# The last two output slabs by token halves, the norm by pairs of chunks, and the next stage's second slab split last

## What is computed

```python
x = x + gate_m * y
h = rmsnorm(x, norm_ffn_g[layer]) * (1.0 + scale_f) + shift_f
x = x + gate_f * swiglu(h, ffn_w_gate[layer], ffn_w_up[layer], ffn_w_down[layer])
```

## Time and profile before

| | us |
|---|---|
| median of three runs | 2349.04 (2347.94 to 2349.14) |
| the profiled execution's own time | 2349.4 |
| its span, first to last instruction | 2347.6 |

### The profile page before, as it was taken

The page is one execution under the profiler, slowest core; times in us unless marked ns, Lnnn a source line. Parts: engine busy times, 40 slices in busy tenths (PEclk is TensorE's granted clock), DMA queues, the critical chain, the costliest instruction groups (busy, mean ns, idle before and its releaser), DMA issues.

```text
span 2347.6 us, 34925 instructions
## 1 busy us (share of the span) xinstructions
PE 2266.1 (97%) x14369; PEld 1920.9 (82%) x14369; DVE 1401.0 (60%) x1800; ACT 1042.5 (44%) x1568; POOL 366.7 (16%) x164
## 2 busy tenths in 40 slices
PE   6999999999999999999999999999999999999998
PEld 4777888878889986668998998888777788898897
DVE  4856755543347765547883676645367345984484
ACT  4546553443215444435552455334255325553352
POOL 0346447347790000000000000000000000000000
PEclk9999999999999999999999999999999999999999
DMA  7433232334452324311333233212211222233232
GB/s 294 143 116 135 100 135 91 118 115 181 181 210 90 109 73 163 130 67 54 109 108 117 83 124 110 85 62 72 90 55 56 89 90 72 91 108 126 90 108 90
DMA packets 40762, 260.56 MB, mean 111 GB/s; under 512 B 4432, under 2 KB 6832, under 8 KB 10416
## 3 DMA queue, kind: packets, MB, share of 16 engines
q1 hardware_dynamic: 40624, 258.59, 30.3%
HBM read 256.42 MB, written 2.15 MB: 110 GB/s over the span
## 4 chain that ended last, share of the span: by engine, by line
PE 79%; DVE 8%; ACT 5%; issue 2%; POOL 2%; DMA 0%; DVEq 0%; ACTq 0%
PE D L301 10%; PE D L303 10%; PE D L302 10%; PE D L1638 7%; PE D L1640 7%; PE D L1639 7%; PE D L1403 2%; PE D L2866 2%; PE D L1405 2%; PE D L1404 2%; DVE lo L366 1%; PE D L2868 1%; PE D L2867 1%; PE D L1422 1%; ACT hi L362 1%
## 5 line engine op out<-in xcount | busy, mean ns | idle before, releaser
L366 DVE TENSOR_TENSOR lo<-raw,hi 128x2048 fp32r<-128x2048 f32 (+3 forms) x131 | 288.9, 2205 | 200.4 <-ACT hi L362 200.2
L362 ACT ACTIVATE hi<-raw 128x2048 fp32r<-128x2048 f32 (+3 forms) x131 | 230.1, 1756 | 328.6 <-PE D L303 240.0
L301 PE MATMUL D<-hH,lo 128*128 128x512 f32 x560 | 227.3, 406 | 5.6 <-DVE lo L366 5.6
L303 PE MATMUL D<-hH,hi 128*128 128x512 f32 x560 | 220.9, 394 | 0.0
L302 PE MATMUL D<-hL,hi 128*128 128x512 f32 x560 | 220.9, 394 | 0.0
L1638 PE MATMUL D<-tH,lo 128*128 128x256 f32 x768 | 216.3, 282 | 0.5 <-issue 0.5
L1640 PE MATMUL D<-tH,hi 128*128 128x256 f32 x768 | 216.3, 282 | 0.0
L1639 PE MATMUL D<-tL,hi 128*128 128x256 f32 x768 | 216.2, 282 | 0.0
L375 POOL TENSOR_TENSOR adar<-adar 128x1024 f32<-128x1024 f32 (+2 forms) x120 | 213.2, 1777 | 9.4
L373 POOL TENSOR_TENSOR adar<-adar,small 128x2048 f32<-128x2048 f32 x40 | 154.0, 3850 | 326.5 <-DVE zi L1289 189.0
L1638 PE MATMUL D<-hH,lo 128*128 128x256 f32 x576 | 162.6, 282 | 2.3 <-ACT D L1721 2.3
(11 more groups left out here) (537 smaller groups left out, 5481.7 us busy)
## 6 DMA issues: line engine op xcount, KB each, us to landing
raw<-in_slabs SPq DMA_DIRECT2D x185, 1024.0 KB, 4.8
adar<-in_ada SPq DMA_DIRECT2D x42, 1024.0 KB, 4.8
fw<-in_ada SPq DMA_DIRECT2D x6, 1024.0 KB, 24.0
x<-in_xin SPq DMA_DIRECT2D x2, 1024.0 KB, 8.9
dt<-bcast SPq DMA_DIRECT2D x8, 256.0 KB, 3.2
dtb<-bcast SPq DMA_DIRECT2D x8, 256.0 KB, 3.5
qd<-bcast SPq DMA_DIRECT2D x8, 256.0 KB, 3.7
out<-x SPq DMA_DIRECT2D x8, 256.0 KB, 2.2
```

The source lines that it names most:

```text
L301: T_.matmul(o, lo[s.slot][:, w], H[:, k, :], start=(k == 0), stop=False)
L303: last = T_.matmul(o, hi[s.slot][:, w], H[:, k, :], start=False, stop=(k == kc - 1))
L362: S_.activation(hi[s.slot][:, 0:n], raw[s.slot][:, 0:n], ACT.Copy).then_inc(hi_ready, 1)
L366: V_.tensor_tensor(lo[s.slot][:, 0:n], raw[s.slot][:, 0:n], hi[s.slot][:, 0:n], ALU.subtract).then_inc(lo_ready, 1)
```

## The change

The last two output slabs of each end (numbers 2 and 3) run by halves, in the order: slab 2 first half, slab 3 first half, slab 2 second half, slab 3 second half. Adds, squares and folds of these slabs go by halves. The sum of the first half stands in slab 2's second half, after 18 of its 48 matmuls, and takes four ones products instead of three. The norm goes by eight pairs of chunks: VectorE multiplies a pair by the root alone, ScalarE applies gain and shift as scale and bias, two activations to hH and two to tR, and tR is written wherever n is not 4; VectorE subtracts hH from tR. At n = 4 there is no tR, and VectorE makes hL chunk by chunk. The first next slab is split inside the norm (behind pair 0 on ScalarE, and behind the adds of slab 2's second half on VectorE). The second is split behind the last pair on both engines. A dummy slab that was loaded and split at the very end is gone. The cut diff (the counters of semaphores are left out):

```diff
-                    pe.wait_ge(h_ready, h_base(hb) + h * KC + k + 1)
+                    pe.wait_ge(h_ready, h_base(hb) + (h * KC + k) // 2 + 1)
...
-                T_.matmul(o, ones, a[:, 0, TH[h]], start=True, stop=False)
                 for m in range(2):
-                    pe.wait_ge(fsq_ready, 10 * f + 6 + 2 * h + m + 1)
+                    T_.matmul(o, ones, a[:, m, TH[h]], start=(m == 0), stop=False)
+                for m in range(2):
+                    pe.wait_ge(fsq_ready, 12 * f + 4 * h + m + 7)
                     last = T_.matmul(o, ones, b[:, m, TH[h]], start=False, stop=(m == 1))
...
             for h in range(2):
...
+                for j in range(N_OUT - 2, N_OUT):
+                    s = Slab(base + j)
+                    if h == 0:
+                        pe.wait_ge(lo_ready, s.plus(1))
+                        pe.wait_ge(bank_free[s.slot], s.prior())
+                    for m in range(2):
+                        o = D[s.slot][:, h, m * HT:(m + 1) * HT]
+                        for k in range(kc):
+                            if (h, j, m * kc + k) == (1, N_OUT - 2, 6):
+                                ones_half(pe, f, 0)
...
+        def half_fold_dve(dve, f, h):
+            dve.wait_ge(fsq_ready, 12 * f + 4 * h + 6)
+            dve.wait_ge(fold_ready, 3 * f + 1)
+            for a, b in sums_of(f):
+                last = V_.tensor_tensor(a[:, :, TH[h]], a[:, :, TH[h]], b[:, :, TH[h]], ALU.add)
+            last.then_inc(fold_ready, 1)
...
+        of_pair = lambda t_, p: t_[:, 2 * (p % 4):2 * (p % 4) + 2, TH[p // 4]]
+        norm_pair = lambda p: nq[:, 2 * (p % 2):2 * (p % 2) + 2, :]
+        whole_pair = lambda p: tR[:, (3, 1, 0, 2)[p // 2], 2 * (p % 2):2 * (p % 2) + 2, :]
+
+        def close_act(act, base, f, n, gain, shift):
+            def pair(p):
+                act.wait_ge(xg_ready, XG[n] + p + 1)
+                for to in (of_pair(hH, p), whole_pair(p)) if n != 4 else (of_pair(hH, p),):
+                    for m in range(2):
+                        c = 2 * (p % 4) + m
+                        last = S_.activation(to[:, m, :], norm_pair(p)[:, m, :], ACT.Identity, bias=shift(c), scale=gain(c))
+                last.then_inc(hh_ready, 1)
             S_.preload_act_table_set("natural_log_exp_and_others")
+            half_squares_act(act, base, f, 0, N_OUT - 1)
             half_rstd_act(act, f, n, 0)
+            pair(0)
+            split_hi(act, Slab(base + N_OUT))
+            half_squares_act(act, base, f, 1, N_OUT - 2)
+            pair(1)
+            pair(2)
+            half_squares_act(act, base, f, 1, N_OUT - 1)
+            pair(3)
+            half_rstd_act(act, f, n, 1)
+            for p in range(4, KC):
+                pair(p)
+            split_hi(act, Slab(base + N_OUT + 1))
...
+            def normed(p):
+                if p >= 2:
+                    dve.wait_ge(h_ready, hb0 + p - 1)
+                V_.tensor_tensor(norm_pair(p), of_pair(x, p), nrs[:, TH[p // 4]].unsqueeze(1).to_broadcast([P, 2, HT]),
+                                 ALU.mult).then_inc(xg_ready, 1)
+
+            def rest(p):
+                dve.wait_ge(hh_ready, hb0 + p + 1)
+                if n != 4:
+                    V_.tensor_tensor(of_pair(hL, p), whole_pair(p), of_pair(hH, p), ALU.subtract).then_inc(h_ready, 1)
...
             half_rstd_dve(dve, n, 0)
+            normed(0)
+            normed(1)
+            rest(0)
+            half_adds_dve(dve, base, gate, f, 1, N_OUT - 2)
+            split_lo(dve, Slab(base + N_OUT))
+            half_fold_dve(dve, f, 1)
+            normed(2)
+            rest(1)
+            normed(3)
+            rest(2)
+            half_adds_dve(dve, base, gate, f, 1, N_OUT - 1)
+            rest(3)
+            half_rstd_dve(dve, n, 1)
+            normed(4)
+            normed(5)
+            rest(4)
+            normed(6)
+            rest(5)
+            normed(7)
+            rest(6)
+            rest(7)
             split_lo(dve, Slab(base + N_OUT + 1))
...
         def last_dve(dve, base, gate, f, n, gain):
...
+            half_rstd_dve(dve, n, 0)
+            scaled(0, range(0, 4))
+            half_adds_dve(dve, base, gate, f, 1, N_OUT - 2)
+            half_fold_dve(dve, f, 1)
+            scaled(0, range(4, KC))
+            half_adds_dve(dve, base, gate, f, 1, N_OUT - 1)
+            half_rstd_dve(dve, n, 1)
+            scaled(1, range(KC))
...
-            alone(G_ROUT, N_SLABS + 1 - G_ROUT)
+            alone(G_ROUT, N_SLABS - G_ROUT)
```

More of the change, by code:

```diff
@@ L282, in build @@
         TH = (slice(0, HT), slice(HT, T))
-        BY_HALF = (2, 3, 5, 6, 8)
-        h_base = lambda hb: sum(2 * KC if b in BY_HALF else KC for b in range(hb)) + (4 if hb > 2 else 0) + (4 if hb > 5 else 0)
-        XG = {0: 0, 1: KC, 2: 3 * KC + 4, 3: 5 * KC + 4, 4: 7 * KC + 8, "x": 9 * KC + 8, 6: 10 * KC + 8, 7: 12 * KC + 12}
+        h_base = lambda hb: KC * hb + (4 if hb > 2 else 0) + (4 if hb > 5 else 0)
+        XG = {0: 0, 1: KC, 2: 2 * KC + 4, 3: 3 * KC + 4, 4: 4 * KC + 8, "x": 5 * KC + 8, 6: 6 * KC + 8, 7: 7 * KC + 12}
         RM = {0: 0, 1: 2, 2: 6, 3: 10, 6: 14, 7: 18}
@@ L594, in final_pe @@
         def final_pe(pe, base, kc, H, L, ready, f, begun=False):
-            for j in range(N_OUT - 1):
+            for j in range(N_OUT - 2):
                 s = Slab(base + j)
@@ L600, in final_pe @@
                     product(pe, s, kc, 2, H, L)
-            s = Slab(base + N_OUT - 1)
-            pe.wait_ge(lo_ready, s.plus(1))
-            pe.wait_ge(bank_free[s.slot], s.prior())
             for h in range(2):
[L605 to L614, removed]
+                for j in range(N_OUT - 2, N_OUT):
[8 more added lines that the diff above has]
+                                ones_half(pe, f, 0)
+                            w = slice((k * 2 + m) * P, (k * 2 + m + 1) * P)
+                            T_.matmul(o, lo[s.slot][:, w], H[:, k, TH[h]], start=(k == 0), stop=False)
+                            T_.matmul(o, hi[s.slot][:, w], L[:, k, TH[h]], start=False, stop=False)
+                            last = T_.matmul(o, hi[s.slot][:, w], H[:, k, TH[h]], start=False, stop=(k == kc - 1))
+                    last.then_inc(slab_done if h else out_half, 1)
         def square_sum(f, to, m, c, cols):
@@ L640, in final_dve @@
                 split_lo(dve, s.next(2))
[L641 to L662, removed]
+            dve.wait_ge(fsq_ready, 12 * f + 4)
+            for a, b in sums_of(f):
+                last = V_.tensor_tensor(a[:], a[:], b[:], ALU.add)
+            last.then_inc(fold_ready, 1)
+            half_adds_dve(dve, base, gate, f, 0, N_OUT - 2)
+            half_fold_dve(dve, f, 0)
+            half_adds_dve(dve, base, gate, f, 0, N_OUT - 1)
         def half_rstd_act(act, f, n, h):
@@ L691, in close_act @@
             S_.preload_act_table_set("natural_log_exp_and_others")
-            half_squares_act(act, base, f, 0)
+            half_squares_act(act, base, f, 0, N_OUT - 1)
             half_rstd_act(act, f, n, 0)
[L694 to L708, removed]
+            pair(0)
@@ L725, in close_dve @@
-        def close_dve(dve, base, gate, f, n, hb, gain, shift):
-            half_adds_dve(dve, base, gate, f, 0)
-            half_rstd_dve(dve, n, 0)
[L729 to L754, removed]
@@ new lines, in close_dve @@
+        def close_dve(dve, base, gate, f, n, hb, gain, shift):
+            hb0 = h_base(hb)
+            def normed(p):
[7 more added lines that the diff above has]
+                    V_.tensor_tensor(of_pair(hL, p), whole_pair(p), of_pair(hH, p), ALU.subtract).then_inc(h_ready, 1)
+                else:
+                    dve.wait_ge(xg_ready, XG[n] + p + 1)
+                    for m in range(2):
+                        c = 2 * (p % 4) + m
+                        last = V_.scalar_tensor_tensor(out=hL[:, c, TH[p // 4]], in0=norm_pair(p)[:, m, :], scalar=gain(c),
+                                                       in1=hH[:, c, TH[p // 4]], op0=ALU.mult, op1=ALU.subtract)
+                    last.then_inc(h_ready, 1)
+            half_rstd_dve(dve, n, 0)
+            normed(0)
[19 more added lines that the diff above has]
+            rest(7)
@@ L3279, in _ @@
             final_act(act, G_ROUT, 4)
-            close_act(act, G_ROUT, 4, 6, zero)
+            close_act(act, G_ROUT, 4, 6, col(vec, V["ln2"]), zero)
             quick_act(act, G_FFN2, 2, 5)
```

72 lines of the change are left out of this document (45 added, 27 removed).

## The result

The changed kernel takes 2359.23 us (median of six runs, 2356.55 to 2361.78) against 2349.09 us for the kernel before (six runs, 2347.53 to 2350.48): a ratio of 1.0045, 95% interval 1.0032 to 1.0058. It is slower by 10.1 us; 9.0 was forecast. Its profiled execution took 2361.1 us with a span of 2359.3.

What follows compares the result with a forecast made beforehand. ScalarE's queue was taken to bound the norm's second half at the ends feeding tR. 3 x 1.8 + 3.9 - 0.1 - 0.2 = +9.0 us gave 2358.0 against the median 2349.04; range 2349.5 to 2361.5.

Steps and rivals of the forecast that it cites:

- The operand: Norm activations on ScalarE get scale beside bias: second per-partition operand costs 0.08 us, step 0.48 instead of 0.40.
- f = 3: Fourth of five stage hand-overs: head wins 1 us, tail gives it back; 47.3 before, 47.2 after, -0.1.
- Rival (a): Second operand on ScalarE's activations is free: +0.9 in sum, 2349.9 us; chance 0.17, with half prices between.
- Rival (b): Back-to-back activations of a pair hide their operands and step 0.32: -5.9, 2343.1 us; chance 0.05.
- The sum at f = 2: Third hand-over: second Exp ends at 31.4, 1 us won; then 12.8 against 9.8, 3 us lost; +1.8.
- f = 0, 2 and 4: First, third and fifth hand-overs, which fed tR already; activation count stays 32; +1.8 us each.
- f = 1: Second hand-over, no tR before: activations double from 16 to 32; 40.3 to 44.15, +3.9, the largest loss.
- The late split: Second next slab's split, moved behind the last pair: 1.9 + 2.3 us that nothing covers, TensorE waiting.
- f = 5: Last end: adds no longer wait behind eight scalings, 0.9 won; TensorE's 0.7 longer way takes most: -0.2.
- The signs named ahead: Profile after: activations 0.57 to 0.58 us; low-part waits about 1.8 or 1.3; second-half by-halves waits, one per pair.

Runs made afterwards that it cites:

- e1: Kernel before, with a scale operand (a column of ones) added to all of the norm's activations, order unchanged: 2357.86 us, ratio 1.0045.
- e3: Changed kernel without the second operand: activations have the shift alone, the gain is left out of the computation: 2348.13 us, ratio 1.0000.
- e5: Changed kernel with f = 1 alone as before: gain on VectorE's multiply, one activation per chunk, no tR: 2355.88 us, ratio 1.0033.
- e9: e7 with the second next slab's split put last again, behind the last pair: 2347.57 us, ratio 0.9996.
- e10: e7 run once more, unchanged: 2342.85 us, ratio 0.9979 against the kernel before.
- e2: Kernel before, with the second next slab's high part moved behind the norm's last piece: 2350.32 us, ratio 1.0007.
- e4: Changed kernel with the last split's high part moved ahead of the squares of the fourth slab's second half: 2352.47 us, ratio 1.0020.
- e6: Changed kernel with one activation per chunk into tR, ScalarE copying the pair to hH, and the early split of e4: 2347.06 us, ratio 0.9994.
- e8: e6 with f = 1 in the form of e5: 2344.84 us, ratio 0.9987 against the kernel before.
- e7: As e6, but VectorE copies the pair from tR to hH, and f = 1 in the form of e5: 2342.48 us, ratio 0.9974.

## Why the prediction came out right

**The operand.** The prediction took 0.08 us for the second operand and a step of 0.48, from the step from none to one. The chain and e1 show 0.09 and 0.49. This is the mis-sized term, by 0.01 on some 24 activations at each of four ends: 0.24 each, 1 us in all, and with it the sum of 9.0 becomes 10.0. The five ends lost 10.9 where 9.2 were put down; this is 1.0 of the 1.7, and f = 3 (below) is the rest. The Trainium skill (ScalarE: Activation LUTs, What ACT_TABLE_LOAD costs) has about 93 ns for each pointer operand, with neighbours overlapping by as much; the trace now agrees for the second one too (0.50 to 0.59 us alone, and a step 0.09 longer). Rival (a), the free operand, falls with e1 and e3: its 2349.9 is close to the 2348.13 that e3 takes with the operand gone. Rival (b) needed a step under 0.33.

**The sum at f = 2.** The second Exp was put at 31.4 after the start; it ends at 1095.92 less 1064.51 = 31.4. From there 12.8 was put down and 12.9 came. The low part of the first next slab was put at 23.2 and ends at 23.3 (1087.86). The +1.8 came out as +1.9, +2.1 and +2.0 at f = 0, 2 and 4; the 0.2 is the operand.

**f = 1.** It was to be the largest loss, +3.9 against +4.2 measured, for the count of activations; e5 shows that the loss is there.

**Without the operand.** The prediction's sums at a step of 0.40 give the five ends +1.15, and e3 has +1.2. Part of this is luck: f = 0, 2 and 4 came out 0.1 to 0.4 lower than put down, and f = 3 0.65 higher.

**f = 3.** This is the end that was wrong: +0.7 for -0.1. The head's gain was taken over from f = 2 as 1 us. By VectorE's and ScalarE's timelines the second root is there 37.9 us after the start in the kernel before and 37.5 after, so only 0.4 was won. Its tail then lost 1.1. The operand (0.6 in e3) and the late split (0.2, e9 against e10) are in that.

**The late split.** The prediction's words for it, that it returns at its end where nothing covers its 1.9 and 2.3 us, describe the waits (1.4 to 1.7 us for the low part, where 1.3 and 1.8 were put) but not the cost. Its sums had taken the split out of the middle of the queue as well, and so were right where the words mislead: e2 shows a cost of nothing in the kernel before where ScalarE's queue is full and 0.6 where it has gaps, e4 and e9 one of 0.6 to 1.0 at most ends. In e4 that is idle time of ScalarE that the split filled, less what the squares come later; in e9 it is VectorE's wait for the late high part.

**f = 5** gave 0.24 for the 0.2 put down. The adds of the last half no longer wait behind eight scalings, as the earlier trace rows had it: before they began 0.97 us after the last product (2338.71 less 2337.74), now they have VectorE to themselves. TensorE's way to that product is 0.6 longer, where 0.7 was put down.

```profile
2346.57 1.67 DVE L801 SCALAR_TENSOR_TENSOR x<-x,vec,nrs 128x256 f32<-128x256 f32 x4
2350.39 0.76 DVE L655 SCALAR_TENSOR_TENSOR x<-D,x 128x256 f32<-128x256 f32 x2 [2.15 <-PE D L615]
```

**The signs named ahead.** Activations of 0.57 to 0.58 us came at 0.59. The waits of one per pair did not come as described: at f = 0, 1, 2 and 4 none stands in the first half of the by-halves product, where the sum's wait for squares took their place (0.6 to 0.7), f = 3 has one of 0.83 there, and in the second half the first pair costs 1.95 and the later ones 0.2 to 0.3 or nothing, for a reason that the last section has.

**What the ends don't hold.** 10.9 at five ends less 0.2 at the last is 10.7, near the 10.1 of the medians. The two profiled executions differ by 11.7. The part between f = 3 and f = 4, where no code differs, took 492.2 us before and 493.7 after. It is 493.9 in e6 and 492.2 in e8 too. Why it takes one or the other wasn't followed up. The other parts took 0.5 less in sum.

## What to carry to other kernels

Before work is moved from one engine to another, price it on the engine that the chain of waits names at that place, not on the one that it makes lighter: here 0.09 us for an operand, 16 to 32 times at each of five ends, was nearly the whole result (9.7 of 10.9 us, e3), while the 2 to 3 us per end that VectorE saved bought nothing. When two results differ only in rounding, make one with operands and copy the pair to the other without; on the engine with room the copy here took 0.42 us. A step at the end of a full queue cost no more here than in its middle (e2). Moved into idle time of its engine it gained, but less than the idle time that it filled: look for what waits for it last (e4: 0.75 of 1.21 us; e9 against e10: 0.73 of 1.8).

## What the runs showed of the hardware

TensorE's clock fell to half behind a long wait, after the work had resumed. The windows of the changed kernel at f = 2 (same columns as above), where TensorE had stood still for 1.95 us until 1099.53:

```profile
1100.00:1101.00 1.00, 1.00 (x11) 1.00 (x9) 0.45 (x2) 1.00 (x3) 0.00 (x0) 1.00 0.00 0
1101.00:1102.00 1.00, 0.77 (x4) 0.51 (x4) 0.97 (x2) 1.00 (x3) 0.00 (x0) 0.50 0.00 0
1102.00:1103.00 1.00, 1.00 (x7) 1.00 (x6) 0.45 (x2) 1.00 (x3) 0.00 (x0) 0.50 0.00 0
1103.00:1104.00 1.00, 1.00 (x6) 1.00 (x6) 0.41 (x1) 1.00 (x3) 0.00 (x0) 0.50 0.05 16
1104.00:1105.00 1.00, 1.00 (x9) 1.00 (x8) 0.31 (x1) 1.00 (x3) 0.00 (x0) 0.79 0.00 0
1105.00:1106.00 1.00, 1.00 (x11) 1.00 (x10) 0.38 (x1) 1.00 (x1) 0.00 (x0) 1.00 0.00 0
```

It is granted 0.50, which is 1.2 GHz, for about 3.4 us, and a product's step grows from 0.119 to 0.214 us. ScalarE is busy all through, and that is why it cost nothing: at f = 0 the wait was as long (1.96), the clock stayed at 1.00, three pairs each cost a wait of 0.27 to 0.29, and the hand-over took 44.49 against 44.33. At f = 2 the slower products filled those waits. In e1 at f = 2 the clock fell as the work resumed, after a wait of 1.81 us, and stayed at 0.50 for about 6.8 us. At f = 3, where TensorE is nearer to the end of the chain, the lower clock shows in the time. e6 and e8 have the same code there. The hand-over of e6:

```profile
1413.22:1460.83 47.61, 43.64 (x321) 41.71 (x320) 30.79 (x49) 27.51 (x49) 0.00 (x0) 0.96 0.26 96
```

In e8 the same stretch is 46.88 us, with TensorE busy for 42.52 and a granted clock of 1.00. So e6 took 0.73 us longer, with the clock at 0.96 in the mean. Both had the same wait of 2.1 us there, so these rows don't show what decides on the fall. The 1.0 us that e4 won at f = 3 (1.00 there, 0.96 in the changed kernel) is therefore mostly the clock and not the split, which e9 against e10 puts at 0.2. In e7, where the longest wait at f = 0, 1, 2 and 4 is 0.74 us, the clock of those ends is 1.00.
